# Modulation columns of two stacked transformer layers: vectors as the stationary side, in four column groups

## The chip, the cores and the metric

One core of a Trainium2 chip runs the whole program. The time is what the device needs for one execution, in microseconds (us). Engines are named as in the profile: PE is TensorE's matmul, PEld its weight loads, DVE is VectorE, ACT is ScalarE, SP issues most DMAs.

## The reference, cut to what matters

Two stacks of two layers each, width D = 1024, 256 latent tokens and (first stack) 256 context tokens, all in float32. In the first stack each layer's norms are scaled, shifted and gated by vectors that come from two conditioning vectors, `c` (latent tokens) and `c_ctx` (context tokens):

```python
silu_c, silu_cc = jax.nn.silu(c), jax.nn.silu(c_ctx)
mod = (silu_c @ w_ada[l] + b_ada[l])                      # 1024 -> 6 * 1024
sh1, sc1, g1, sh2, sc2, g2 = jnp.split(mod, 6, axis=-1)
mod_c = silu_cc @ w_ada[l][:, :n_cm * D] + b_ada[l][...]  # n_cm = 6 in layer 0, 2 in layer 1
hc = _modulate(xc, mod_c[0], mod_c[1])                    # norm(x) * (1 + scale) + shift
xc = _post(xc, yc, mod_c[2], ...)                         # residual with a gate
```

`w_ada` has 48 chunks of 128 output columns a layer. The change concerns how these products are made. All else (projections, gated linear attention, attention, convolution, feed-forward, the second stack) is the same computation before and after.

## The kernel before, in words

Activations lie transposed: channels on partitions, 256 tokens along the free side. Weights come as a stream of 723 loads of 8 tiles of 128x128 (SP, three landing buffers `w_raw`). ACT copies each to `w_hi`, rounded to the fast fp32r format; DVE makes `w_lo = w_raw - w_hi`. Each dense product is three matmuls (hi*hi, hi*lo, lo*hi; L489 to L491), so a load is 24 of them. SP refills a `w_raw` buffer when DVE has made its `w_lo`. A dense product of 8 tiles ends in one of four PSUM banks, which ACT evacuates (`arrived`, `moved`).

All order is written out by hand: each engine's block runs the same list of units, counted by semaphores. The first stack is done in four passes ("turns"): layer 0 context (turn 0), layer 0 latent (1), layer 1 context (2, only its keys, values and state), layer 1 latent (3). A full turn goes: projections; `gla`, 17 steps (`STEPS`), in each of which DVE and ACT prepare decays and PE makes a product of them (L739); heads; `attention`; output merges; `residual`; two norms; `feed_forward` in two halves ("up" chunks, then "down"). "Fill" units are put between the dependent steps so that PE has work: `gla_fill`, `key_fill`, `attention_fill`, `out_fill`, `norm_fill`.

The modulation columns before come in three ways:

* **Units** ("ada", 58 of them, and 8 at the start). One 128-column chunk of `w_ada` (512 KB, one buffer `a_raw`) is the stationary side, the two vectors `cvec` (128x2) the moving side: 8 fp32 products of 128x128 weights with 2 columns (L539; each is 2 weight loads and 2 matmuls). ACT copies 128x2 from PSUM to `mod` (L1293) and then issues the DMA for the next chunk (L1296). Their numbers by stage are the tuple `counts` in `ada_units`: turn 0 has 14 in `gla`, 3 at the heads, 8 in attention, 4 in the output, 3 in the norms; turn 1 has 12 in attention, 3 in the norms; turn 3 has 8 and 3.
* **Rows** (38). In the feed-forwards of turns 0 and 1, DVE multiplies a chunk of `w_ada` stored by output column (128x1024) with the conditioning vector repeated on all partitions, and sums (L1815). ACT issues their loads (`row_load`).
* **The first 16 chunks**, needed before the first product can start: 8 as units from 8 loads, and two groups of 4 chunks on DVE, which multiplies and adds `a_group` by each vector's element (L2081, L2084), then PE sums over partitions (`first_sums`, L550).

`pending` and `modulation()` on DVE add the bias and 1.0 later. `CONV_PLACES` are the places in turn 0's feed-forward at which DVE does pieces (of 24) of turn 1's convolution ahead of time; a piece is ten tap instructions (L1869).

## Time and profile before

| | us |
|---|---|
| Median of 3 runs | 3044.44 (3039.38 to 3047.6) |
| The profiled execution's own time | 3033.33 |
| Its span, first to last instruction | 3031.6 |
| PE busy | 2838.8 (94%) |
| DVE busy | 2204.4 (73%) |
| ACT busy | 1514.1 (50%) |
| Granted TensorE clock, mean | 0.955 of full speed |

The spans of PE's instructions overlap, as a matmul's record runs on for a while after the next has begun; what one costs PE is read from start to start. A releaser in brackets (`<-DVE ...`) names what ended an idle time.

### The profile page before, as it was taken

To read this page: it belongs to the slowest core of one execution; us is meant where nothing else is said; L and a number is where in the kernel's file an instruction comes from. 1 tells how busy PE (TensorE), PEld (TensorE's weight loads), DVE (VectorE), ACT (ScalarE), POOL (GpSimd) and SP (SyncE) were. 2 spreads that over 40 slices of the span, in tenths; PEclk is the share of its full clock that TensorE was granted. 3 is DMA by queue.
4 is the path that set the end of the run, shared out by engine and by line. 5 is a ranking of instruction groups with operands and counts; after the bars stand their busy time and mean duration, and the time that the engine had idled before them with its cause. 6 is when DMAs were issued, how large, how long until landed. Compare 5 with 4: busy or idle time off the path is not lost.

```text
span 3031.6 us, 54592 instructions
## 1 busy us (share of the span) xinstructions
PE 2838.8 (94%) x21440; PEld 2716.1 (90%) x21440; DVE 2204.4 (73%) x3798; ACT 1514.1 (50%) x3111; POOL 0.2 (0%) x4
## 2 busy tenths in 40 slices
PE   8999999999999999999989998999999889997998
PEld 7999889899989889889989997888998779995998
DVE  6976777678889876867767898867666665566655
ACT  3644345454565335445564653454555455555554
POOL 0000000000000000000000000000000000000000
PEclk7999999999999989989999999999999899998999
DMA  7542444456742333447733423335553325541554
GB/s 265 157 160 94 146 133 153 152 176 222 232 137 91 105 124 127 143 169 236 232 117 118 143 76 118 111 125 179 166 183 117 105 81 187 185 140 52 160 185 153
DMA packets 123335, 451.45 MB, mean 149 GB/s; under 512 B 13744, under 2 KB 15792, under 8 KB 122464
## 3 DMA queue, kind: packets, MB, share of 16 engines
q1 hardware_dynamic: 108704, 393.30, 40.2%
q10 hardware_dynamic: 14400, 54.86, 5.3%
q8 instruction: 171, 2.80, 0.4%
q14 instruction: 60, 0.49, 0.1%
HBM read 447.05 MB, written 1.05 MB: 148 GB/s over the span
## 4 chain that ended last, share of the span: by engine, by line
PE 65%; DVE 22%; ACT 6%; DMA 4%; issue 2%; SPq 0%; ACTq 0%; DVEq 0%
PE lin L489 15%; PE lin L490 15%; PE lin L491 15%; DVE arena L1869 5%; DVE w_lo L1692 5%; DMA w_raw<-in_stream 3%; PE lin L539 3%; PE aux L604 2%; ACT w_hi L1078 2%; PE aux L739 1%; DVE rstd L1717 1%; PE aux L651 1%; PE aux L672 1%; PE aux L595 1%; PE lin L517 1%
## 5 line engine op out<-in xcount | busy, mean ns | idle before, releaser
L1692 DVE TENSOR_TENSOR w_lo<-w_raw,w_hi 128x1024 fp32r<-128x1024 f32 x722 | 875.2, 1220 | 321.3 <-ACT w_hi L1078 314.9
L489 PE MATMUL lin<-h_hi,w_hi 128*128 128x256 f32 x3456 | 997.3, 289 | 5.2 <-ACT arena L1346 2.9
L1078 ACT ACTIVATE w_hi<-w_raw 128x512 fp32r<-128x512 f32 x1446 | 828.7, 623 | 323.8 <-DMA w_raw<-in_stream 232.8
L490 PE MATMUL lin<-h_lo,w_hi 128*128 128x256 f32 x3456 | 985.7, 285 | 0.0
L491 PE MATMUL lin<-h_hi,w_lo 128*128 128x256 f32 x3456 | 985.4, 285 | 0.0
L489 PEld LDWEIGHTS lin<-h_hi,w_hi 128*128 128x128 f32 x3456 | 672.2, 195 | 9.9 <-ACT arena L1346 4.9
L490 PEld LDWEIGHTS lin<-h_lo,w_hi 128*128 128x128 f32 x3456 | 671.9, 194 | 0.5
L491 PEld LDWEIGHTS lin<-h_hi,w_lo 128*128 128x128 f32 x3456 | 671.1, 194 | 0.0
L489 PE MATMUL lin<-s_hi,w_hi 128*128 128x256 f32 x1520 | 450.6, 296 | 26.6 <-DVE s_lo L1778 23.2
L490 PE MATMUL lin<-s_lo,w_hi 128*128 128x256 f32 x1520 | 441.0, 290 | 0.0
L491 PE MATMUL lin<-s_hi,w_lo 128*128 128x256 f32 x1520 | 440.0, 289 | 0.0
L489 PEld LDWEIGHTS lin<-s_hi,w_hi 128*128 128x128 f32 x1520 | 302.4, 199 | 36.2 <-DVE s_lo L1778 28.0
L490 PEld LDWEIGHTS lin<-s_lo,w_hi 128*128 128x128 f32 x1520 | 303.2, 199 | 1.1 <-issue 0.5
L491 PEld LDWEIGHTS lin<-s_hi,w_lo 128*128 128x128 f32 x1520 | 302.9, 199 | 0.0
L1869 DVE SCALAR_TENSOR_TENSOR arena<-arena,vec 128x256 f32<-128x256 f32 x720 | 290.2, 475 | 0.0
L1795 DVE SCALAR_TENSOR_TENSOR X<-X,gate_buf 128x256 f32<-128x256 f32 x120 | 50.9, 425 | 142.1 <-ACT gate_buf L1238 56.9
L539 PEld LDWEIGHTS lin<-cvec,a_raw 128*128 128x128 f32 x928 | 116.5, 202 | 11.5 <-DMA a_raw<-in_ada 8.9
L539 PE MATMUL lin<-cvec,a_raw 128*128 128x2 f32 x928 | 114.5, 254 | 7.1 <-DMA a_raw<-in_ada 7.0
L1717 DVE RECIPROCAL rstd<-std 128x256 f32<-128x256 f32 (+1 forms) x34 | 59.5, 1751 | 83.8 <-ACT std L1107 83.8
L1224 ACT ACTIVATE gate_buf<-lin 128x256 f32<-128x256 f32 x110 | 41.7, 379 | 102.6 <-PE lin L491 86.3
L517 PE MATMUL lin<-w_hi,h_hi 128*128 128x256 f32 x320 | 90.8, 284 | 1.5 <-ACT arena L1313 1.5
L519 PE MATMUL lin<-w_lo,h_hi 128*128 128x256 f32 x320 | 90.6, 283 | 0.0
(278 smaller groups left out, 3858.9 us busy)
## 6 DMA issues: line engine op xcount, KB each, us to landing
w_raw<-in_stream SPq DMA_DIRECT2D x723, 512.0 KB, 3.5
a_raw<-in_ada ACTq DMA_DIRECT2D x58, 512.0 KB, 3.4
arena<-in_rows ACTq DMA_DIRECT2D x38, 512.0 KB, 5.1
arena<-in_first SPq DMA_DIRECT2D x2, 2048.0 KB, 19.6
X<-in_tokens SPq DMA_DIRECT2D x2, 1024.0 KB, 14.6
s_f<-in_ada SPq DMA_DIRECT2D x4, 512.0 KB, 10.3
arena<-in_ada SPq DMA_DIRECT2D x4, 512.0 KB, 17.2
arena<-in_const ACTq DMA_DIRECT2D x1, 1856.0 KB, 7.9
```

Source lines behind the costliest of these rows:

```text
L489: used(pe.matmul(o, whi, hi[:, k, :], start=k == 0, stop=False), first)
L490: pe.matmul(o, whi, lo[:, k, :], start=False, stop=False)
L491: mm = pe.matmul(o, wlo, hi[:, k, :], start=False, stop=k == kcs - 1)
L517: mm = pe.matmul(o[:, 0:2 * P], xhi, whi, start=k == 0, stop=False)
L519: pe.matmul(o[:, 0:2 * P], xhi, wlo, start=False, stop=False)
L539: mm = pe.matmul(o[:, 0:2], w[:, k, :], cvec[:, k, :], start=k == 0, stop=k == KC - 1)
L604: mm = pe.matmul(aux[1][:, 0:S], c1("mean1024"), squares[:, k, :], start=k == 0, stop=k == KC - 1)
L1078: act.activation(w_hi[:, slot, part], w_raw[:, raw, part], ACT.Copy).then_inc(sems["hi_ready"], 1)
L1692: dve.tensor_tensor(w_lo[:, m % SLOTS, :], w_raw[:, m % RAW, :], w_hi[:, m % SLOTS, :].bitcast(F32), ALU.subtract).then_inc(sems["lo_ready ...
L1717: step(dve.reciprocal(r, std[0:rows, slot, :]))
L1795: dve.scalar_tensor_tensor(x[:, c, :], x[:, c, :], alpha, gate_buf[:, c % 2, :], ALU.mult, ALU.add).then_inc(sems["r_ready"], 1)
L1869: dve.scalar_tensor_tensor(CV[:, c, :], YP[:, c, tap:tap + S], v1(l, "conv_w", c * TAPS + tap), CV[:, c, :], ALU.mult, ALU.add).then_inc(s ...
```

## The change: what it does, and the diff

**The unit is turned round.** The stationary side is now `cvec`, padded from 2 to 32 columns (zeros), and the moving side is the 128x128 tile of `w_ada`. The 8 products go in turn to four groups of 32 output partitions of one bank (`g = k % GROUPS`), so each group holds the partial sum of two of them, as rows: partitions 32g and 32g+1 hold the two vectors' results. ACT copies these 128x128 to `ada_part`. A second product, `ada_sum`, with `ada_part` as the stationary side and `pick` (128x2, ones at rows 32g and 32g+1) as the moving side, adds the four groups and turns the rows into columns. It is written into the same bank at columns 256 and 257 ahead of the *next* unit, and that unit's evacuation first copies it to `mod`. A unit "sum" closes a turn's series.

**No rows.** The 38 row products, their loads, `c_rows` and `row_bias` are gone. Layer 1's 48 chunks are all units. There are 80 units after the start: turn 0 has 14, 4, 10, 4 (gla, heads, attention, output), turn 1 has 14, 4, 10, 4, turn 3 has 8, 0, 8, 0. The norms hold none; turns 1 and 3 have 5 idle matmuls (`keep_clock(IDLE // 2)`) at two places in them. The second vector's columns of layer 1 are made together with the first's, where before chunks 0 to 15 were loaded for each.

**The start.** All 16 first chunks are four groups of four, each in two DMAs of 1 MB: PE multiplies `cvec` into four column groups with 512 moving columns (`first_ada`), ACT copies 128x512, PE sums with `pick`. The order is shift chunks 0 to 3, scale 8 to 11, shift 4 to 7, scale 12 to 15. The first `w_raw` load is issued ahead of the last group, the other two behind it, and `vec1` ahead of all groups. ACT and DVE work on the first four channels' chunks while the other groups arrive.

**Around turn 0's norm.** The modulated input of the next pass is made in two halves, after output chunks 4 and 5, and half of its low parts after chunk 6. Turn 0's feed-forward takes 8 convolution pieces, not 6.

```diff
-                  ("head128", -(-(KVH + HEADS) // GROUPS) * GROUP), ("head256", GROUP), ("alpha", 2)):
+                  ("head128", -(-(KVH + HEADS) // GROUPS) * GROUP), ("head256", GROUP), ("alpha", 2), ("pick", 2)):
...
-ROW_LAT, ROW_CTX = 2 * HALF, 2 * KC
-ROW_ITEMS = ROW_LAT + ROW_CTX
-ROW_BUFS = 3
-ROW_TURNS = {0: (CTX, range(0, ROW_CTX)), 1: (LAT, range(ROW_CTX, ROW_ITEMS))}
-
-
...
-CONV_PLACES = [(0, "up", 3), (0, "up", 5), (0, "up", 7), (0, "up", 9), (1, "up", 1), (1, "up", 10)]
+CONV_PLACES = [(0, "up", 3), (0, "up", 6), (0, "down", 1), (0, "down", 4), (1, "up", 1), (1, "up", 4), (1, "up", 7), (1, "down", 1)]
...
+ADA_COUNTS = {(0, CTX): (14, 4, 10, 4), (0, LAT): (14, 4, 10, 4), (1, LAT): (8, 0, 8, 0)}
...
-    counts = {(0, CTX): (14, 3, 8, 4, 3), (0, LAT): (0, 0, 12, 0, 3), (1, LAT): (0, 0, 8, 0, 3)}[l, s]
...
+FIRST_GROUPS = (0, 8, 4, 12)
+FIRST_CHUNKS = 4
...
-            for g, (c, k) in enumerate(FIRST_GROUPS):
-                for u in range(4 * g, 4 * g + 4):
-                    sp.dma_start(a_first[u], ada_in[u]).then_inc(first_landed[g], 16)
-                sp.dma_start(a_group[g], first_in[:, g, :, :]).then_inc(group_landed[g], 16)
-            for s in range(RAW):
+            sp.dma_start(vec1[:, :, :], vec1_in).then_inc(sems["vec_landed"], 16)
+            for g in range(len(FIRST_GROUPS)):
+                if g == len(FIRST_GROUPS) - 1:
+                    sp.dma_start(w_raw[:, 0, :], stream[0]).then_inc(landed[0], 16)
+                for i in range(2):
+                    sp.dma_start(a_group[g][i], first_in[:, g, i * (KC // 2):(i + 1) * (KC // 2), :]).then_inc(group_landed[g][i], 16)
+            for s in range(1, RAW):
                 sp.dma_start(w_raw[:, s, :], stream[s]).then_inc(landed[s], 16)
-            sp.dma_start(vec1[:, :, :], vec1_in).then_inc(sems["params"], 16)
...
+            def ada_sum(o):
+
+                pe.wait_ge(sems["lin_evac"], ada_open.pop())
+                return pe.matmul(o[:, S:S + 2], ada_part[:, :], c1("pick"), start=True, stop=True)
 
             def ada(unit):
 
-                k0 = len(ada_done)
-                ada_done[unit] = k0
-                if k0 < len(FIRST_UNITS):
-                    w = a_first[k0]
-                    if k0 % 4 == 0:
-                        pe.wait_ge(first_landed[k0 // 4], 4 * 16)
-                else:
-                    w = a_raw
-                    pe.wait_ge(sems["ada_landed"], 16 * (k0 - len(FIRST_UNITS) + 1))
+                ada_done.append(unit)
+                o = bank()
+                if ada_open:
+                    ada_sum(o)
+                pe.wait_ge(sems["ada_landed"], 16 * len(ada_done))
+                for k in range(KC):
+                    g = k % GROUPS
+                    mm = pe.matmul(o[g * GROUP:(g + 1) * GROUP, 0:P], cvec[:, k, :], a_raw[:, k, :], start=k < GROUPS, stop=k >= KC - GROUPS)
+                done(mm)
+                ada_open.append(n.at("lin_done"))
+
+            def first_ada(g):
+
                 o = bank()
                 for k in range(KC):
-                    mm = pe.matmul(o[:, 0:2], w[:, k, :], cvec[:, k, :], start=k == 0, stop=k == KC - 1)
+                    if k % (KC // 2) == 0:
+                        pe.wait_ge(group_landed[g][k // (KC // 2)], 16)
+                    q = k % GROUPS
+                    mm = pe.matmul(o[q * GROUP:(q + 1) * GROUP, :], cvec[:, k, :], a_group[g][k // (KC // 2)][:, k % (KC // 2), :],
+                                   start=k < GROUPS, stop=k >= KC - GROUPS)
                 done(mm)
-
-            def first_sums(g):
-
-                _, k = FIRST_GROUPS[g]
-                pe.wait_ge(sems["part_ready"], 2 * g + 2)
+                return n.at("lin_done")
+
+            def first_sums(g, partial):
+
+                pe.wait_ge(sems["lin_evac"], partial)
                 o = bank()
-                for c in range(k):
-                    for st, part in enumerate(first_parts[g]):
-                        at_col = 2 * c + st
-                        mm = pe.matmul(o[:, at_col:at_col + 1], part[:, c * P:(c + 1) * P], c1("mean1024")[:, 0:1],
-                                       start=True, stop=True)
+                for c in range(FIRST_CHUNKS):
+                    mm = pe.matmul(o[:, 2 * c:2 * c + 2], first_parts[g][:, c * P:(c + 1) * P], c1("pick"), start=True, stop=True)
                 done(mm)
 
...
-                        for u in FIRST_UNITS[0:4]:
-                            unit(l, s, u)
+                        first = first_ada(0)
                         variance(M)
-                        first_sums(0)
-                        for u in FIRST_UNITS[4:8]:
-                            unit(l, s, u)
-                        first_sums(1)
-
-                        pe.wait_ge(sems["glr_split"], at.up("glr_split", 2))
+                        second = first_ada(1)
+                        first_sums(0, first)
+                        first_sums(1, second)
+                        for g in (2, 3):
...
                     else:
-                        unit(l, s, beside[0])
+                        keep_clock(IDLE // 2)
                         variance(M)
-                        unit(l, s, beside[1])
+                        keep_clock(IDLE // 2)
                         layernorm(x, "x_ready")
-                        unit(l, s, beside[2])
                         keep_clock(IDLE)
                     n.up("h_ready", KC)
...
-                    if ahead and c == 5:
+                    if ahead and c == (4 if next_high else 5):
...
+                    if next_high and c == 6:
+                        high_parts(next_high, early, "early_ready", n_hi)
...
-            def row_load(r):
-                act.dma_start(a_rows[r % ROW_BUFS], rows_in[r]).then_inc(rows_landed[r % ROW_BUFS], 16)
-
...
+            def ada_fetch():
+
+                if len(ada_moved) < len(ADA_LATER):
+                    act.dma_start(a_raw[:, :, :], ada_in[len(ada_moved)]).then_inc(sems["ada_landed"], 16)
+
+            def ada_column(o):
+
+                l, c = ada_moved[-1]
+                return act.activation(mod[:, l, c, :], o[:, S:S + 2], ACT.Copy)
+
+            def ada(l, c, first):
+                o = arrived(0)
+                if not first:
+                    ada_column(o)
+                moved(act.activation(ada_part[:, :], o[:, 0:P], ACT.Copy))
                 ada_moved.append((l, c))
-                if len(ada_moved) < len(ADA_LATER):
-                    act.dma_start(a_raw[:, :, :], ada_in[len(FIRST_UNITS) + len(ada_moved)]).then_inc(sems["ada_landed"], 16)
+                ada_fetch()
...
+                first_part(0)
                 root(aux[1])
+                first_part(1)
+                first_columns(0)
+                first_columns(1)
+                split_to(1)
+                high_parts(lambda c: mod[:, 0, c, 0:1], chunks=range(0, 4))
+                for g in (2, 3):
+                    first_part(g)
+                    first_columns(g)
+                split_to(2)
+                high_parts(lambda c: mod[:, 0, c, 0:1], chunks=range(4, KC))
+                ada_fetch()
                 split_to(RAW)
-                first_chunks(*FIRST_GROUPS[0], float(D))
-                for _, (_, c) in FIRST_UNITS[4:8]:
-                    first_chunks(c, 1, 1.0)
+                act.wait_ge(sems["vec_landed"], 16)
                 act.wait_ge(sems["params"], PARAMS)
                 act.activation(wglr_hi[:, :], wglr[:, :], ACT.Copy).then_inc(sems["glr_split"], 1)
...
-            def row_product(turn, r):
-
-                st, rows = ROW_TURNS[turn]
-                c = r - rows[0]
-                dve.wait_ge(rows_landed[r % ROW_BUFS], 16 * (r // ROW_BUFS + 1))
-                dve.wait_ge(sems["row_used"], r + turn + 1)
-                dve.scalar_tensor_tensor(row_products, a_rows[r % ROW_BUFS], 1.0, c_rows[:, :], ALU.mult, ALU.mult,
-                                         accum_out=mod[:, 1, c:c + 1, st]).then_inc(sems["row_used"], 1)
...
+                dve.wait_ge(sems["vec_landed"], 16)
+                shift, scale = lambda c: mod[:, 0, c, 0:1], lambda c: mod[:, 0, 8 + c, 0:1]
+                pending.extend((0, c, 3) for c in range(0, 4))
+                pending.extend((0, c, 4) for c in range(8, 12))
+                modulation()
+                dve.wait_ge(sems["xc_ready"], at.now("xc_ready"))
+                for c in range(0, 4):
+                    scale_chunk(W, scale, c)
+                    if c >= 1:
+                        low_part(c - 1, shift)
+                low_part(3, shift)
+                lows(1)
+                pending.extend((0, c, 6) for c in range(4, 8))
+                pending.extend((0, c, 8) for c in range(12, 16))
+                modulation()
+                for c in range(4, KC):
+                    scale_chunk(W, scale, c)
+                lows(2)
+                for c in range(4, KC):
+                    low_part(c, shift)
+                n.up("lin_evac", 2 * len(FIRST_GROUPS))
                 dve.wait_ge(sems["params"], PARAMS)
-                step(dve.tensor_copy(masks[:, :, :], stage[:, :, :]))
                 dve.wait_ge(sems["glr_split"], at.up("glr_split"))
...
+                            if turn == 0 and c in (4, 5):
+                                dve.wait_ge(sems["xc_ready"], at.now("xc_ready"))
+                                for k in range(4 * c - 16, 4 * c - 12):
+                                    scale_chunk(early, lambda k: mod[:, nl, 8 + k, ns:ns + 1], k, early, "early_ready")
...
+                                for k in range(4):
+                                    low_part(k, next_shift, early, n_hi, n_lo)
...
+    c["pick"] = np.tile(np.eye(GROUP)[:, 0:2], (GROUPS, 1))
```

The start on PE, before. `s_f` and `arena` hold chunks of `w_ada`, `gate_buf` and `y_buf` DVE's partial sums; L502 is the first dense product:

```order
L595 MATMUL aux<-X,const 128x256 x8
L539 MATMUL lin<-cvec,s_f 128x2 x32
L604 MATMUL aux<-M,const 128x256 x8
L550 MATMUL lin<-const,gate_buf 128x1
L550 MATMUL lin<-const,y_buf 128x1
...
L539 MATMUL lin<-cvec,arena 128x2 x32
L550 MATMUL lin<-const,s_f 128x1 x8
L502 MATMUL lin<-h_hi,w_hi 128x256
```

And after (L525 is `first_ada`, L535 `first_sums`, L476 the first dense product):

```order
L581 MATMUL aux<-X,const 128x256 x8
L525 MATMUL lin<-arena,cvec 32x512 x8
L590 MATMUL aux<-M,const 128x256 x8
L525 MATMUL lin<-arena,cvec 32x512 x8
L535 MATMUL lin<-const,gate_buf 128x2 x4
L535 MATMUL lin<-const,y_buf 128x2 x4
L525 MATMUL lin<-s_f,cvec 32x512 x8
L535 MATMUL lin<-const,s_f 128x2 x4
L525 MATMUL lin<-arena,cvec 32x512 x8
L535 MATMUL lin<-const,s_f 128x2 x4
L476 MATMUL lin<-h_hi,w_hi 128x256
```

The 64 narrow products (32 and 32) are gone; four rounds of 8 wide products have come, and the last round and its sums stand ahead of the first dense product.

A step of `gla` in turn 1 on PE, before: a dense product's end (L491), the decay product (L739), and the next dense product:

```order
L491 MATMUL lin<-h_hi,w_lo 128x256
L739 MATMUL aux<-arena 128x128 x8
L489 MATMUL lin<-h_hi,w_hi 128x256
L490 MATMUL lin<-h_lo,w_hi 128x256
L491 MATMUL lin<-h_hi,w_lo 128x256
```

And after (L725 is the decay product, L503 `ada_sum`, L514 the turned unit):

```order
L465 MATMUL lin<-h_hi,w_lo 128x256
L725 MATMUL aux<-arena 128x128 x8
L503 MATMUL lin<-const,ada_part 128x2
L514 MATMUL lin<-a_raw,cvec 32x128 x8
L725 MATMUL aux<-arena 128x128 x8
L463 MATMUL lin<-h_hi,w_hi 128x256
```

Units have come into these steps, and one step holds a unit and no dense product between two decay products.

## Rows read from the trace of the kernel before

**Rows 1.** The page, chain that ended last: shares by engine.

```profile
PE 65%; DVE 22%; ACT 6%; DMA 4%; issue 2%; SPq 0%; ACTq 0%; DVEq 0%
```

**Rows 2.** Windows, five filled stages: span, busy us (count) by engine, clock, DMA.

```profile
180.19:276.00 95.81, 93.39 (x764) 91.48 (x763) 67.47 (x95) 40.10 (x75) 0.00 (x0) 0.98 0.41 137
883.27:977.11 93.84, 86.30 (x705) 84.85 (x704) 86.80 (x126) 51.14 (x82) 0.00 (x0) 0.96 0.37 119
362.87:440.00 77.13, 69.48 (x522) 66.75 (x523) 66.82 (x159) 34.44 (x92) 0.00 (x0) 0.93 0.42 138
1066.61:1169.60 102.99, 97.85 (x681) 87.22 (x681) 76.13 (x188) 41.06 (x110) 0.00 (x0) 0.91 0.38 123
1889.00:1986.50 97.50, 89.58 (x616) 78.43 (x616) 75.93 (x189) 40.81 (x106) 0.00 (x0) 0.92 0.33 108
```

**Rows 3.** Timeline, PE (start us, us, line): steps of turns 0, 1.

```profile
205.11 2.03 PE L739 MATMUL aux<-arena 128*128 128x128 f32 x16
...
209.85 1.84 PE L539 MATMUL lin<-cvec,a_raw 128*128 128x2 f32 x16
211.56 2.03 PE L739 MATMUL aux<-arena 128*128 128x128 f32 x16
...
910.88 1.95 PE L739 MATMUL aux<-arena 128*128 128x128 f32 x16
...
915.54 1.95 PE L739 MATMUL aux<-arena 128*128 128x128 f32 x16
```

**Rows 4.** Timeline, PE: eight products into four column groups, and neighbours.

```profile
300.26 0.28 PE L491 MATMUL lin<-h_hi,w_lo 128*128 128x256 f32 x1
300.47 1.07 PE L625 MATMUL aux<-arena,const 128*32 128x256 f32 x16
301.47 0.39 PE L489 MATMUL lin<-h_hi,w_hi 128*128 128x256 f32 x1
301.69 0.28 PE L490 MATMUL lin<-h_lo,w_hi 128*128 128x256 f32 x1
```

**Rows 5.** Timeline, PE: eight full-width fp32 products, the next behind.

```profile
447.05 3.62 PE L595 MATMUL aux<-arena,const 128*128 128x256 f32 x16
450.32 0.47 PE L489 MATMUL lin<-h_hi,w_hi 128*128 128x256 f32 x1
```

**Rows 6.** Groups by line, ACT: us, mean ns of evacuations, narrow and wide.

```profile
L1293 ACT ACTIVATE mod<-lin 128x2 f32<-128x2 f32 x58 | 9.9, 170 | 38.2 <-PE lin L539 38.1
...
L1273 ACT ACTIVATE a_hi<-aux 128x128 fp32r<-128x128 f32 x32 | 8.7, 270 | 7.5 <-PE aux L672 7.5
```

**Rows 7.** Source of a_raw's loads: from issue to landing.

```profile
DMA to landing us min/median/max: 3.2/3.4/8.9
```

**Rows 8.** Timeline of the start, all engines.

```profile
10.55 5.12 PE L595 MATMUL aux<-X,const 128*128 128x256 f32 x16 [10.55 <-DMA const<-in_const]
...
25.61 6.10 PE L604 MATMUL aux<-M,const 128*128 128x256 f32 x16
...
33.26 13.21 PE L539 MATMUL lin<-cvec,arena 128*128 128x2 f32 x64
33.44 2.42 ACT L1078 ACTIVATE w_hi<-w_raw 128x512 fp32r<-128x512 f32 x4 [1.30 <-DMA w_raw<-in_stream]
...
52.87 0.55 PE L502 MATMUL lin<-h_hi,w_hi 128*128 128x256 f32 x1 [2.99 <-DVE h_lo L1739]
```

**Rows 9.** Groups by line, DVE: the row products.

```profile
L1815 DVE SCALAR_TENSOR_TENSOR arena<-arena 128x1024 f32<-128x1024 f32 x38 | 46.3, 1219 | 0.2
```

**Rows 10.** Windows in the feed-forwards of turns 1 and 3.

```profile
1353.00:1403.00 50.00, 47.95 (x388) 47.74 (x387) 37.41 (x57) 25.03 (x52) 0.00 (x0) 0.97 0.77 267
...
2153.00:2203.00 50.00, 50.00 (x419) 50.00 (x418) 30.03 (x43) 24.31 (x50) 0.00 (x0) 1.00 0.59 181
```

**Rows 11.** Timeline, PE: the wait before turn 0's norm.

```profile
568.04 1.22 PE L693 MATMUL aux<-std,const 128*128 128x256 f32 x2 [5.52 <-DVE std L1800]
```

**Rows 12.** The chain in order of time, turn 3's norms: start us, us, what.

```profile
2098.07 8.92 DMA a_raw<-in_ada
```

254 lines of the change are left out of this document (79 added, 175 removed).

## The prediction

> **What bounds the kernel now.** I read the chain that ended last first, then PE by stage in windows, then single steps in the timeline. In the chain PE has 65%, DVE 22%, ACT 6% and DMA 4% [rows 1]: mostly PE's own work sets the end, in places DVE's. The windows say where. In turn 0's `gla` (first row) PE is busy 93.4 of 95.8 us and DVE 67.5; in turn 1's (second) PE 86.3 of 93.8 and DVE 86.8; in the three attentions PE is busy 90 to 95% and DVE 74 to 87% [rows 2]. The reader should see that the difference between turns 0 and 1 is the units: from one decay product to the next there are 6.45 us in turn 0 (205.11 to 211.56) and 4.66 us in turn 1 (910.88 to 915.54), and a unit takes 1.71 us from its start to the next start (209.85 to 211.56) [rows 3]. So a unit in `gla` is paid in full, and taking it away stops paying at about 4.7 us a step, where DVE is as full as PE.
>
> **The price of a turned unit.** Nothing in the trace has this shape, so I bound it. Eight products into four column groups with 256 moving columns take 1.00 us from start to next start (300.47 to 301.47), where eight of full width with the same columns take 3.27 (447.05 to 450.32) [rows 4, 5]: four groups do run side by side. Half the columns can't cost more: upper end 1.00; if the array sets it, 3.27/4/2 = 0.41, the lower end. I take 0.54, nearer the low one, since 1.00 is 0.82 of columns plus about 0.13 to empty the array. A normal start comes 0.12 after the last (419 in 50 us [rows 10]). Entering takes 0.21 (300.26 to 300.47), 0.09 more, and from the first product behind to its successor it is 0.22 (301.47 to 301.69), 0.10 more [rows 4]. `ada_sum` is one narrow product, 1/8 of an old unit, 0.21 [rows 3]. Together 0.95 us, with bounds 0.8 and 1.4, against 1.71.
>
> In the Trainium skill, TensorEngine Tiling (Array Packing), Tiling Modes, says that a change of tiling mode drains TensorE. The two transitions of rows 4, 0.09 and 0.10 us, agree with it, and they speak against this change, which makes 160 of them. Without a drain the sum would be some 15 us lower.
>
> **The sum, part by part** (against the profiled execution, 3033.3 us with a span of 3031.6).
>
> *Start.* The first dense product starts at 52.87, behind DVE's sums and the last narrow ones [rows 8]. Now it needs the four groups. From 10.55 to 33.4 about 9 MB landed (two sets of four loads of 0.5 MB, two of 2 MB, one of the stream, one of `a_raw`), 0.39 MB a us [rows 8]; so behind `vec1` (0.36 MB) the groups are complete at about 17, 22 and 27, the first stream load at 29, the last group at 34. A `first_ada` is twice the 256-column row, 2 us at the full clock and 4 at half; the clock is at half where the variance of 3.27 us at full takes 6.1 [rows 5, 8]. Last group 34, product to 37, copy and sums to 39 or 41, bias, scale, high part to 42, and the second chunk's weights wait for `w_lo` of load 1, which DVE makes behind four scales: 44 to 48. I take 46: **-7** us (bounds -12 and +2: the groups stand on PE ahead of the first dense product, and stream loads 1 and 2 come behind 8 MB).
>
> *Turn 0.* 32 units before and after, all in stages that PE fills: 32 x (1.71 - 0.95) = -24. Two steps of `gla` hold only a unit (the order of the part above); there DVE has its decays to make and to place whatever PE does (they are most of the 4.66 us that fill it in turn 1), so a shorter unit is not a shorter step: +3. **-21.**
>
> *Turn 1.* 22 units are new in `gla`, heads and output: 22 x 0.95 = +21, not hidden, as PE has no free time there [rows 2, 3]. Attention goes from 12 to 10 units: 12 x 1.71 - 10 x 0.95 = 11, of which I take 8.5, since its shortest items wait for the softmax. Steps with a unit alone: +2.5. Four units at the output lie one dense product apart (24 starts, 2.9 us) and a load of `a_raw` takes 3.4 us, up to 8.9 [rows 7]; behind a waiting unit stands the whole of PE: +2. The norm without its three units -2, two convolution pieces less on DVE -1. **+14.**
>
> *Turn 3.* 8 units in `gla` +7.6, four of them alone in a step +4, attention 8 x 0.76 = 6, taken as -4. In the norm the chain runs 8.92 us through a load of `a_raw` [rows 12]; it goes, and what is late next is the root and the reciprocal of the same norm, so -3. **+4.5.**
>
> *Feed-forwards.* The 38 row products, 46.3 us of DVE [rows 9], lie beside PE's work and are not saved as such. What they and their loads cost is seen in turn 1: 388 matmuls in 50 us at 267 GB/s, against 419 at 181 GB/s in turn 3 [rows 10]; 31 matmuls are 3.7 us. Turn 0 has 16 of the rows but gets two convolution pieces more. -4 and -2: **-6**, bounds 0 and -10.
>
> *Before turn 0's norm* PE stands 5.52 us for the last channel sum, which waits behind the early scaling on DVE [rows 11]; that work now comes in halves: **-2.**
>
> ACT: a unit was one copy of 0.17 us; it is now a 128x128 copy (nearest row 0.27) and a column copy of 0.17 [rows 6]. 80 x 0.44 - 58 x 0.17 = 25 us more, hidden, as ACT is busy only 40 to 55% of these stages [rows 2]; without cover it would be those 25 us. Eight MB less are loaded; DMA bounds none of these stages, so nothing.
>
> Sum: -7 - 21 + 14 + 4.5 - 6 - 2 = -17.5 us. The profiled execution would take 3016. It lies 11 us below the median of the runs, 3044.4, so for the median I forecast 3044.4 - 17.5 = **3027 us**.
>
> **The rivals.**
>
> *A, cheap units.* The unit costs 0.8, the short steps cost nothing since DVE works ahead, and the start is at 43: -12, -9 and -3 more, -41.5 in all: 3003. For it: the groups of rows 4 start side by side. Against: the drains in the same rows. Chance 0.20.
>
> *B, slower.* The turned unit costs as much as the 256-column row, 1.00 + 0.21 + 0.19 = 1.4: because each of the short products pays the array's filling, not its columns. Its place is all 80 units; 80 x 0.45 = +36, so +18.5: 3063. It decides from a unit of 0.95 + 17.5/80 = 1.17 us on. For it: 16 loads and matmuls a unit as before, and more units in turns 1 and 3, where PE has no room [rows 3]. Against: 1.00 us is mostly columns. Chance 0.12.
>
> *C, no change.* What sets the steps with units is then not PE but the way through ACT: evacuate the unit, then the exponential, then DVE's decay, then the product. With a longer evacuation PE's saving is not passed on: turn 0 saves 8 instead of 21, the attentions 4 instead of 12.5: +21.5, so +4: 3048. For it: DVE is at 92% in the second window, and ACT takes its work in order. Against: turn 0's steps show PE back to back with units of 1.71 [rows 3]. Chance 0.20.
>
> By TensorEngine Tiling (Array Packing), PSUM Bottleneck, in the Trainium skill, tiling speeds up TensorE but not the evacuation of PSUM, which may become the bottleneck. That is C; ACT's busy share of rows 2 is against it, its order in the chain for it.
>
> *D, the start does not move.* PE waits for the fourth group and its sums and then for `w_lo`, and begins at 53 all the same; the rest is as forecast: -10.5, 3034. Chance 0.08.
>
> **How the numbers follow.** The forecast has 0.40, with its own range 3012 to 3040. Taking in most of A, C and part of B, the range is 3000 to 3052. A measurement of this kernel can tell about 0.3%, 9 us: faster is below 3035, slower above 3054. Faster: 0.36 of the forecast, all of A, 0.03 of C, 0.05 of D: 0.64. Same: 0.04, 0.15 of C, 0.02 of B, 0.03 of D: 0.24. Slower: 0.10 of B, 0.02 of C: 0.12.
>
> **What would show it.** Start to next start of a unit with its sum: 0.95 (B: 1.4). Steps of turn 0's `gla` 5.7 us instead of 6.45, of turn 1's 5.6 instead of 4.66; C has turn 0's at over 6. First dense product at 44 to 48. Turn 1's feed-forward at 419 matmuls in every 50 us. No load of `a_raw` in the chain of turn 3's norm. The prediction is wrong if the unit is above 1.17 or the steps with a unit alone lose far more than 1 to 1.5 us each.

## The result, and the profile after

The changed kernel takes 2990.4 us (median of 4 runs, 2989.6 to 2994.7) against 3043.0: ratio 0.9829, interval 0.9801 to 0.9858. A second set gave 2994.7 (5 runs) against 3041.3 (17 runs), 0.984, interval 0.9821 to 0.9859. So it is faster by 47 to 53 us. The forecast was 3027 us, range 3000 to 3052: the direction was right, the size not, and the time lies below the range. The profiled execution took 2994.69 us (span 2992.9, mean granted clock 0.965, was 0.955), 38.6 us less than that of before.

The chain of waits that ended last, by engine, has hardly moved against [rows 1]; 39 us went out of a program with the same limits:

```profile
PE 66%; DVE 22%; ACT 7%; DMA 4%; issue 2%; SPq 0%; ACTq 0%; DVEq 0%
```

The unit in turn 1's `gla`, timeline of PE after (start us, us, line, and so on), where [rows 3] had steps of 4.66 without a unit and 6.45 with one:

```profile
884.75 0.28 PE L503 MATMUL lin<-const,ada_part 128*128 128x2 f32 x2
884.96 0.64 PE L514 MATMUL lin<-a_raw,cvec 128*32 128x128 f32 x16
885.54 2.05 PE L725 MATMUL aux<-arena 128*128 128x128 f32 x16
...
890.29 0.28 PE L503 MATMUL lin<-const,ada_part 128*128 128x2 f32 x2
890.50 0.64 PE L514 MATMUL lin<-a_raw,cvec 128*32 128x128 f32 x16
891.08 2.05 PE L725 MATMUL aux<-arena 128*128 128x128 f32 x16
```

The second product takes 0.21 us (884.75 to 884.96), the eight turned ones 0.58, a step 5.54 (885.54 to 891.08). Against 4.66 a unit costs 0.88 us in a step; the old one cost 6.45 - 4.66 = 1.79.

Windows of the stages that the prediction speaks of, before and then after (window, its us, busy us of PE, PEld, DVE, ACT and POOL with counts, granted clock, DMA share, GB/s). In order: turn 0 from the gates to the attention, turn 0's feed-forward, turn 1 from the gates to the attention, turn 1's attention, the end of turn 1 with its norms, turn 3 from the gates to the attention.

```profile
121.30:362.90 241.60, 226.43 (x1738) 217.91 (x1737) 182.33 (x301) 116.83 (x219) 0.00 (x0) 0.94 0.41 135
607.40:835.70 228.30, 224.15 (x1835) 223.41 (x1834) 181.47 (x306) 119.55 (x240) 0.00 (x0) 0.99 0.65 210
853.90:1066.60 212.70, 195.02 (x1469) 184.84 (x1468) 190.58 (x328) 113.34 (x201) 0.00 (x0) 0.96 0.33 107
1066.60:1175.50 108.90, 103.75 (x729) 93.13 (x730) 78.98 (x192) 45.32 (x114) 0.00 (x0) 0.91 0.37 121
1259.20:1310.00 50.80, 42.73 (x245) 38.84 (x243) 32.05 (x56) 21.56 (x47) 0.00 (x0) 0.83 0.33 108
1677.45:1889.10 211.65, 194.24 (x1469) 184.16 (x1468) 191.79 (x329) 111.35 (x195) 0.00 (x0) 0.96 0.35 113
```

```profile
109.90:335.90 226.00, 208.49 (x1788) 196.05 (x1787) 181.27 (x300) 118.73 (x237) 0.00 (x0) 0.95 0.45 147
571.40:791.50 220.10, 219.67 (x1819) 219.05 (x1818) 171.64 (x294) 118.98 (x238) 0.00 (x0) 1.00 0.57 178
809.70:1033.10 223.40, 207.01 (x1792) 193.84 (x1791) 191.27 (x328) 118.15 (x236) 0.00 (x0) 0.98 0.45 145
1033.10:1129.80 96.70, 88.33 (x717) 74.52 (x718) 70.95 (x172) 46.25 (x122) 0.00 (x0) 0.95 0.38 125
1213.80:1261.70 47.90, 40.35 (x307) 36.15 (x305) 32.25 (x57) 22.72 (x54) 0.00 (x0) 1.00 0.39 125
1626.90:1851.80 224.90, 203.95 (x1611) 191.41 (x1610) 192.49 (x330) 114.05 (x210) 0.00 (x0) 0.95 0.39 125
```

The reader should see three things. From the gates to the attention turn 0 lost 18 us of PE's work and 15.6 us of time, and 17 old units and 18 new ones at 1.79 and 0.88 us make 14.6: there the price is paid in full. In turn 1 22 units went in, yet from the gates to the attention the stage grew by 10.7 us only, and the attention shrank by 12.2. And turn 0's feed-forward shrank by 8.2 us where PE's work shrank by 4.5: waiting went too.

The whole program by stages, each from the start of one product on PE to the start of the next: the gates (L700), the scores (L637), the channel sum before a norm (L679), the last variance of the norm (L590); an attention ends where the output's first mean (L581) starts. In us, from one profile of each kernel; `before 2` and `after 2` are the same programs again. The other columns are experiments below, each a change to the changed kernel: the old shape of the unit, turn 1 without its 22 units, the convolution's pieces at the six places of before, no idle products in the norm, and the even spread.

| stage | before | before 2 | after | after 2 | old shape | 22 units out | 6 places | no idle | even |
|---|---|---|---|---|---|---|---|---|---|
| start to the gates | 121.3 | 121.4 | 109.9 | 108.9 | 109.3 | 110.0 | 110.0 | 109.7 | 109.8 |
| turn 0 to its norm | 446.7 | 447.4 | 430.5 | 430.6 | 454.7 | 431.0 | 430.7 | 430.9 | 427.5 |
| its norm | 39.3 | 39.3 | 31.0 | 30.4 | 30.4 | 30.4 | 31.0 | 31.0 | 30.4 |
| its feed-forward | 228.3 | 230.8 | 220.1 | 219.4 | 219.4 | 220.1 | 226.6 | 219.6 | 219.4 |
| turn 1, gates to attention | 212.7 | 211.7 | 223.4 | 224.5 | 243.8 | 212.2 | 222.9 | 224.2 | 223.8 |
| its attention | 108.8 | 108.4 | 96.7 | 96.7 | 101.3 | 96.1 | 98.9 | 96.6 | 95.4 |
| its output | 111.5 | 111.1 | 115.6 | 115.3 | 120.6 | 111.1 | 114.9 | 115.8 | 115.0 |
| its norms | 23.0 | 22.5 | 16.3 | 16.3 | 18.0 | 19.2 | 18.0 | 19.2 | 18.0 |
| its feed-forward | 212.3 | 212.6 | 211.0 | 211.1 | 208.3 | 211.0 | 209.9 | 211.0 | 209.8 |
| turn 3, gates to attention | 211.7 | 211.7 | 224.9 | 224.9 | 226.9 | 224.8 | 223.1 | 224.9 | 215.4 |
| turn 3, rest before the feed-forward | 226.6 | 229.6 | 222.6 | 222.6 | 225.4 | 222.7 | 222.4 | 222.5 | 223.2 |

What is left out (turn 2, turn 3's feed-forward, the second stack) stays within 4 us; 3 of them separate the two profiles of the changed kernel, in the second stack, which takes 717 us in one and 714 in the other.

### The profile page after: what moved, and what is told of

It reads as the page before. It is cut to its first block, busy times and chain, and to the rows that moved or that the text cites. A ratio compares the mean times of both kernels' runs of the same rounds, so it can differ in the third digit from the quotient of the medians.

```text
span 2992.9 us, 55534 instructions
## 1 busy us (share of the span) xinstructions
PE 2784.5 (93%) x21928; PEld 2632.6 (88%) x21928; DVE 2142.9 (72%) x3688; ACT 1527.2 (51%) x3209; POOL 0.2 (0%) x4
## 4 chain that ended last, share of the span: by engine, by line
PE 66%; DVE 22%; ACT 7%; DMA 4%; issue 2%; SPq 0%; ACTq 0%; DVEq 0%
PE lin L463 16%; PE lin L464 16%; PE lin L465 16%; DVE arena L1818 6%; DVE w_lo L1668 4%; DMA w_raw<-in_stream 3%; PE aux L590 2%; ACT w_hi L1060 2%; PE aux L725 2%; DVE rstd L1693 1%; PE lin L476 1%; PE aux L581 1%; PE lin L479 1%; PE lin L480 1%; PE aux L658 1%
## 5 line engine op out<-in xcount | busy, mean ns | idle before, releaser
L1187 ACT ACTIVATE y_buf<-lin 128x256 f32<-128x256 f32 x110 | 41.9, 381 | 110.4 <-PE lin L465 110.4
L491 PE MATMUL lin<-w_hi,h_hi 128*128 128x256 f32 x320 | 90.8, 284 | 1.8 <-ACT arena L1284 1.8
L725 PE MATMUL aux<-arena 128*128 128x128 f32 x672 | 84.4, 279 | 8.7 <-DVE arena L1968 8.6
L725 PEld LDWEIGHTS aux<-arena 128*128 128x128 f32 x672 | 78.5, 192 | 13.8 <-DVE arena L1968 11.8
```

Source lines behind the costliest of these rows:

```text
L491: mm = pe.matmul(o[:, 0:2 * P], xhi, whi, start=k == 0, stop=False)
L725: mm = pe.matmul(pair[kt][:, h * P:(h + 1) * P], part, part, start=True, stop=True)
```

## The experiments

Theory: the turned unit pays because its products run side by side, and most of what the forecast missed lies in turn 1, where units filled stretches in which PE stood or ran at half clock, and in places that have nothing to do with units. Each edit is against the changed kernel, unless it says otherwise.

**The changed kernel again.**

> The changed kernel as it is, so that its spread between executions is known beside the others of this set, and whether the 52.6 us between the two medians stand against the 38.6 us between the two profiled executions. If the profiled execution of the kernel before was only at the lower end of its own spread, the median comes out at 2988 to 2993 us and the ratio at 0.982 to 0.984. If instead the first comparison was an outlier, the ratio comes out at 0.987, which is the ratio of the two profiled executions.

2994.7 us (2988.6 to 2995.5), ratio 0.984. The first comparison was no outlier. Of the nine executions of this kernel five take 2988.6 to 2990.6 us and four 2994.7 to 2995.5, so its median comes out as 2990.4 or 2994.7. The differences below are taken from 2994.7; against the lower value a loss is 4 us larger and a gain 4 us smaller. The profile of before, 3033.3 us, lies below all 17 timed executions of this set (3034.5 to 3049.1); that is most of the gap between 38.6 and 47.

**The old shape of the unit.**

```
-  mm = pe.matmul(o[g*GROUP:(g+1)*GROUP, 0:P], cvec[:, k, :], a_raw[:, k, :], start=k < GROUPS, stop=k >= KC - GROUPS)
+  mm = pe.matmul(o[:, 0:2], a_raw[:, k, :], cvec[:, k, 0:2], start=k == 0, stop=k == KC - 1)
   (no partial copy, no second product)
```

> The changed kernel with its 80 later units in the old shape (eight products of 128x128 weights with two moving columns, no partial copy, no second product); start, counts, places and norms stay. Theory P (a unit's time is paid in full on TensorE, and the turned unit costs 0.79 us against 1.71): 80 x 0.92 = +74 us, 3064 us. Theory H (paid in gla, heads and output, 52 units, but in the attentions, 28 units, half of it lies beside the softmax): 52 x 0.92 + 28 x 0.46 = +61 us, 3051 us, with turn 0's attention nearly unchanged at 84 us. Theory C (the price hardly counts, other parts of the change gave the time): below +40 us.

3050.0 us (12 runs), 1.003 of before (1.0017 to 1.0043): 55 us lost, and with them the whole gain. Theory H was nearly right. Where it shows: turn 0 24 us for 32 units (29 at 0.91 each), turn 1 up to the attention 20.4 for 18 (16.4 at 0.91; the granted clock there is 0.95 against 0.98), its attention 4.6 for 10, the attention of turn 3 2.8 for 8, and in turn 3 up to the attention only 2.0 for 8, so what these eight cost there is not their length. So in the attentions the 0.91 is worth 0.46 in turn 1, 0.35 in turn 3 and nothing that can be seen in turn 0 (86.8 against 83.9 and 87.5).

**All products of a unit in one column group.**

```
-  pe.matmul(o[g*GROUP:(g+1)*GROUP, 0:P], cvec[:, k, :], ...)
+  pe.matmul(o[0:GROUP, 0:P], cvec[:, k, :], ...)
   (the copy and the second product read these 32 rows alone)
```

> The changed kernel with the eight products of each later unit all in the first column group, one behind the other into the same 32 rows (the second product then reads those 32 rows alone); number, shape, loads and order of the products stay. Theory G (the 0.57 us of a unit's eight products come from four groups running side by side; alone, a product of 128 moving columns takes what the decay products show, 0.11 us for each of its two parts, so 1.75 us in all): +1.18 us x 80 = +94 at full price, of which 60 to 100% show: 3050 to 3085 us. Theory W (the products are short because only 32 columns of the stationary side are loaded; the groups matter little): +0.1 us x 80: 2990 to 3000 us.

3059.7 us (5 runs), ratio 1.0063 (1.0048 to 1.0078): theory G. Timeline of PE in turn 1's `gla` of this kernel:

```profile
893.53 1.95 PE L725 MATMUL aux<-arena 128*128 128x128 f32 x16
895.41 0.38 PE L503 MATMUL lin<-const,ada_part 32*128 32x2 f32 x2
895.72 1.94 PE L514 MATMUL lin<-a_raw,cvec 128*32 128x128 f32 x16
900.55 1.95 PE L725 MATMUL aux<-arena 128*128 128x128 f32 x16
```

The median from the first to behind the last of the 16 records is 1.86 us, against 0.57 in four groups: same products, loads and count, 3.2 times as long. A unit costs 7.02 - 4.66 = 2.36 us in a step here, 0.57 more than in the old shape, and 80 of them are only 9.7 us slower than that: the time does not rise in proportion to the unit. The mean granted clock is 0.970 here and 0.963 in the old shape; how much of it this is stays open.

**Turn 1 without its 22 units.**

```
-  ADA_COUNTS = {(0, CTX): (14, 4, 10, 4), (0, LAT): (14, 4, 10, 4), ...
+  ADA_COUNTS = {(0, CTX): (14, 4, 10, 4), (0, LAT): (0, 0, 10, 0), ...
   (it leaves these 22 chunks out; they are zero)
```

> The changed kernel without the 22 units that turn 1 took over (14 in gla, 4 in the heads, 4 at the output); it leaves their 22 chunks of the second layer's modulation out, which are zero. Prediction's price: 22 x 0.95 + 2.5 + 2 = -25 us. Theory P (their price alone, 0.79): 22 x 0.79 = -17 us, 2975 us. Theory F (in gla they fill stretches in which TensorE stands or runs at half clock, so they cost less than their price, 10.7 for 18 and 3.8 for 4): -12 to -15 us, 2978 us, with turn 1's gla and heads at 211 to 214 us and the granted clock there back at 0.96.

2979.7 us, 15.0 less: theory F. 11.2 us for 18 units up to the attention, 0.62 each, where their price of 0.88 would be 15.8, and 4.5 for 4 at the output; the norm lost 2.9 again, with its idle products in place. Two windows show where the 18 are cheap, 13 steps of `gla` before and the same 13 after. DVE is busy through the whole of the first, PE 61.91 of 63.90 us, and PE waits for DVE's decays in two of the steps, 0.99 us each (one is shown below the windows). Most other steps of before run back to back on PE, and there a unit costs its 0.88 (5.54 against 4.66; 0.76 in the last ones, which take 4.78 without it). The window of after has eleven units, but it also has one dense product fewer (2.96 us), since the new spread puts that one ahead of the first step; so the eleven cost 5.1 + 2.96 = 8.1 us, 0.73 each.

```profile
906.10:970.00 63.90, 61.91 (x520) 61.04 (x520) 63.90 (x95) 32.80 (x54) 0.00 (x0) 1.00 0.34 108
```

```profile
865.00:934.00 69.00, 67.48 (x696) 64.99 (x695) 64.36 (x95) 34.59 (x73) 0.00 (x0) 1.00 0.53 176
```

```profile
944.99 2.05 PE L739 MATMUL aux<-arena 128*128 128x128 f32 x16 [0.99 <-DVE arena L2018]
```

The rest is saved ahead of these steps and behind them. Over the whole stage PE stands 18.0 us without the 22 units and 16.4 with them, and the granted clock is 0.96 against 0.98 of 212 and 223 us, which is worth 3 to 4 us. So about a third of the 4.6 us is standing, and the rest fits the half clock.

**The convolution's pieces at the six places of before.**

```
-  CONV_PLACES = [(0, "up", 3), (0, "up", 6), (0, "down", 1), (0, "down", 4), (1, "up", 1), (1, "up", 4), ...
+  CONV_PLACES = [(0, "up", 3), (0, "up", 5), (0, "up", 7), (0, "up", 9), (1, "up", 1), (1, "up", 10)]
```

> The changed kernel with the convolution's pieces in the feed-forward of turn 0 at the six places of before instead of eight, so that two pieces, 20 operations of 0.477 us or 9.5 us of VectorE, go back to turn 1's attention. Theory D (VectorE sets turn 1's attention): that attention goes from 96.7 back to 102 to 104 us, the feed-forward gains 0 to 1, in all +5 to +7 us: 2996 us. Rival (the pieces fit in VectorE's idle time, and the 12.2 us that this attention gained are all from the units): 0 +-2 us, 2990 us.

3000.2 us (2993.3 to 3004.9), 0.9858 against 0.984, so +5.6 us as forecast, but for another reason: the attention lost 2.2 us where theory D had 5 to 7, and turn 0's feed-forward, which was to gain, lost 6.5. PE's waits in this feed-forward, here, and before, in the kernel as changed (line waited for: us in total, times, longest):

```profile
PE lin L463 <- DVE s_lo L1754: 4.7, 1, 4.7
```

```profile
PE lin L489 <- DVE s_lo L1778: 4.2, 1, 4.2
```

```profile
PE lin L476 <- DVE h_lo L1715: 0.4, 1, 0.4
```

DVE's timeline of before at that wait shows a piece ahead of the last of the up half's outputs:

```profile
696.54 4.04 DVE L1869 SCALAR_TENSOR_TENSOR arena<-arena,vec 128x256 f32<-128x256 f32 x10
700.50 2.35 DVE L1692 TENSOR_TENSOR w_lo<-w_raw,w_hi 128x1024 fp32r<-128x1024 f32 x2
702.77 0.42 DVE L1845 TENSOR_TENSOR y_buf<-gate_buf,y_buf 128x256 f32<-128x256 f32 x1
703.23 0.29 DVE L1777 CAST s_hi<-y_buf 128x256 fp32r<-128x256 f32 x1
703.55 0.43 DVE L1778 TENSOR_TENSOR s_lo<-y_buf,s_hi 128x256 fp32r<-128x256 f32 x1
```

The 4.2 us of standing are followed by a stretch at half clock (0.78 and 0.88 in the two 10 us from 697.4 on).

**Before without its row products and their loads.**

```
-  dve.scalar_tensor_tensor(row_products, a_rows[...], 1.0, c_rows[:, :], ..., accum_out=mod[:, 1, c:c + 1, st])
+  dve.tensor_copy(mod[:, 1, c:c + 1, st], a_rows[...][:, 0:1])
   (only the first three loads of each turn stay; the 38 columns are not computed)
```

> The kernel before with its 38 row products on VectorE replaced by copies of one column, and with only the first three loads of each turn; it leaves the computation of those 38 columns of the modulation out. Theory R (the prediction's: the rows and their loads cost the feed-forwards 6 to 10 us): turn 0's feed-forward from 228 to 220 to 223, turn 1's from 212 to 208: 3032 us. Theory C (the 8.2 us that turn 0's feed-forward gained come from where the convolution's pieces stand, as the run with six places says; rows cost next to nothing): both feed-forwards within 2 us, 3038 to 3042 us.

3038.3 us, 0.9989 (0.9976 to 1.0003). Turn 0's feed-forward 228.1, turn 1's 211.1: theory C. 38 products, 46 us of DVE [rows 9], cost nothing that can be measured as long as the wait for `s_lo` stands.

**The changed kernel with the rows kept on VectorE**, so without the 22 units.

```
-  ADA_COUNTS = {..., (0, LAT): (14, 4, 10, 4), (1, LAT): (8, 0, 8, 0)}
+  ADA_COUNTS = {..., (0, LAT): (0, 0, 10, 0), (1, LAT): (8, 0, 8, 0)}
+  (row_load, row_product and row_bias as before the change, at the places of before)
```

> The changed kernel with its turned units, start, places and norms, but the 38 row products on VectorE and their loads kept as before the change, so that turn 1 takes over none of the 22 units (26 units of the second layer: ten in turn 1's attention, eight in gla and eight in the attention of turn 3). Theory R0 (rows on VectorE cost the feed-forwards nearly nothing, as their removal from the kernel before moved it by 0.1%, and the 22 units cost 15 us): 2979.7 + 0 to 3 = 2980 to 2983 us, both feed-forwards within 2 us of 220 and 211. Rival R1 (with eight convolution pieces beside them VectorE or the loads become late in turn 0's feed-forward): it goes to 225 to 228: 2986 to 2990 us.

2993.4 us, 0.9842: R1 by its cause, but above its 2986 to 2990. The 15 us that the units' absence gives are eaten by the feed-forwards, 229.8 us in turn 0 and 219.6 in turn 1. The second does not come back in the run with the units in the attentions alone, which has the same rows (209.5); its cause stays open. PE's waits in turn 0's:

```profile
PE lin L483 <- DVE w_lo L1711: 4.4, 2, 3.4
PE lin L483 <- DVE s_lo L1797: 1.9, 1, 1.9
```

**Before with one piece moved off the hand-over.**

```
-  ... (0, "up", 7), (0, "up", 9), (1, "up", 1), (1, "up", 10)]
+  ... (0, "up", 7), (1, "up", 0), (1, "up", 1), (1, "up", 10)]
```

> The kernel before with one of the convolution's six pieces moved: from behind the tenth chunk of the first up half, (0, up, 9), where VectorE's 4.0 us stand ahead of the last s_lo that TensorE waits 4.2 us for, to behind the first chunk of the second, (1, up, 0). Rows, loads and everything else stay. Theory W (that wait, with the half clock behind it, is the 8.2 us which turn 0's feed-forward gained; the removed row products have no part in it): this feed-forward from 228.3 to 220 to 222 us, the whole 3040 - 7 = 3033 us. Rival V (with the rows VectorE is too full, and the wait comes back at the other hand-over or for w_lo, as in the run that keeps the rows and has eight pieces): 226 to 230 us there, 3038 to 3042 us in all.

3041.3 us, 0.9989 (0.9974 to 1.0004): rival V by its time and its stage, 226.0 us. The wait for `s_lo` halved (2.0 us), 0.6 us for `w_lo` came, and nothing is left in the median.

So turn 0's feed-forward has four corners: rows and six places 228 to 231 us; no rows and six places 227 to 228; rows and eight places 230 to 231; no rows and eight places 219 to 221. With either edit alone PE still waits for DVE, 4 to 8 us in all; only both together free it. Neither the rows nor the places can be called the cause by themselves.

**Without the idle products in the norm of turns 1 and 3.**

```
-  keep_clock(IDLE // 2)
   variance(M)
-  keep_clock(IDLE // 2)
```

> The changed kernel without the ten idle products (five ahead of the variance, five behind it) in the first norm of turns 1 and 3. Theory K (they keep TensorE's granted clock at 1.00 through that norm, where it was 0.64 before the change, and that is most of the 6.7 us that turn 1's norm gained): turn 1's norm goes from 16.3 us to 20 or more, the clock there to 0.7, in turn 3 less: +5 to +8 us, 2997 us. Rival (the norm got shorter because three units of 3.3 us at half clock left it): 0 to -1 us, 2990 us.

2999.2 us, 0.9856: +4.5, nearer theory K than its rival, but its place holds for turn 1 only (16.3 to 19.2 us; in turn 3 nothing moves), and the clock falls to 0.86 and 0.75 in the two halves, not to the 0.61 and 0.69 of before. The first half of turn 1's norms, the kernel as changed and then this one:

```profile
1245.40:1256.50 11.10, 8.49 (x39) 7.16 (x39) 9.88 (x19) 3.41 (x7) 0.00 (x0) 1.00 0.16 48
```

```profile
1246.00:1258.30 12.30, 6.09 (x18) 4.38 (x18) 9.84 (x19) 3.36 (x7) 0.00 (x0) 0.86 0.17 46
```

**The start in another order.** ScalarE's copy of the third group ahead of its split of the first stream load, the second split ahead of the fourth group's copy.

```
-  split_to(1); high_parts(..., chunks=range(0, 4)); [first_part(g); first_columns(g)] for g in (2, 3); split_to(2)
+  first_part(2); split_to(1); high_parts(..., chunks=range(0, 4)); first_columns(2); split_to(2); first_part(3); first_columns(3)
   VectorE:
-  lows(1) ... scale_chunk of 4 to 7; lows(2)
+  lows(2) ... scale_chunk of 4 to 7
```

> The changed kernel with another order at the start: ScalarE copies the third group's partial sums before it splits the first stream load, and splits the second stream load before the fourth group's copy; VectorE makes the second w_lo before the second half of the scales. Theory O (what bounds the start is the order of work on ScalarE and VectorE behind stream load 0, which lands at 26.8): TensorE's wait of 4.5 us ahead of the third group's sums goes, the fourth group's product starts when its load lands, near 31, and the wait of 2.9 us for w_lo goes: the low-rank product's gates start 3 to 5 us earlier than 109 to 110 us; 2987 us. Rival L (the fourth group's load lands only at about 33, so that nothing moves but idle time): 0 to -1 us.

2992.6 us, 0.9843: no difference in the median; the gates start 1.8 to 2.7 us earlier (107.2), and turn 0 up to its norm takes 432.9 us instead of 430.5, so the gain is gone there. Both theories were half right: the wait of 4.51 us for ScalarE is gone, and the fourth group's load takes its place. Timeline of PE after, then in this run:

```profile
25.56 1.07 PE L525 MATMUL lin<-s_f,cvec 128*32 128x512 f32 x8 [0.44 <-DMA s_f<-in_first]
31.14 1.87 PE L535 MATMUL lin<-const,s_f 128*128 128x2 f32 x8 [4.51 <-ACT s_f L1391]
32.94 3.64 PE L525 MATMUL lin<-arena,cvec 128*32 128x512 f32 x16
37.29 1.05 PE L535 MATMUL lin<-const,s_f 128*128 128x2 f32 x8 [0.72 <-ACT s_f L1391]
...
41.73 0.58 PE L476 MATMUL lin<-h_hi,w_hi 128*128 128x256 f32 x1 [2.93 <-DVE w_lo L1668]
```

```profile
30.17 1.94 PE L525 MATMUL lin<-arena,cvec 128*32 128x512 f32 x8 [2.04 <-DMA arena<-in_first]
32.57 1.94 PE L525 MATMUL lin<-arena,cvec 128*32 128x512 f32 x8 [0.46 <-DMA arena<-in_first]
35.54 1.86 PE L535 MATMUL lin<-const,s_f 128*128 128x2 f32 x8 [1.03 <-ACT s_f L1391]
37.27 0.56 PE L476 MATMUL lin<-h_hi,w_hi 128*128 128x256 f32 x1
```

**An even spread in `gla`.**

```
-  steps = spread(gla_fill(l, s), STEPS)
+  steps = [a + b for a, b in zip(spread([dense ones], STEPS), spread([units], STEPS))]
```

> The changed kernel with gla's fill spread in another way: the 16 dense products over the 17 steps as before the change, and the units over the steps by themselves, instead of both in one row that is cut in 17 (which gives turn 3 steps with two dense products beside steps with a unit alone). Theory S (of the 13.3 us that turn 3's gla and heads lost, the 8 units' own 6.3 are a half; the rest is one more dense product ahead of the first decay product, at half clock, and steps with a unit alone, where TensorE waits): turn 3's gla and heads from 224.9 to 217 to 220, turns 0 and 1 change by less than 2: 2986 to 2990 us against 2994.7. Rival (the sum of the work in gla sets its length however it is spread): within 1.5 us.

2978.4 us, 0.9798 (0.9779 to 0.9817): 16.3 us less, more than theory S. Turn 3 gave 9.5 us, turn 0, which theory S left out, 3.1 to 4.5; the stages thus show 13 to 14, and the rest lies within the kernel's two medians. Turn 3 from the gates to the first whole decay step, in the changed kernel and in this one:

```profile
1626.87:1686.67 59.80, 53.24 (x385) 50.94 (x385) 44.48 (x67) 37.85 (x67) 0.00 (x0) 0.86 0.47 151
```

```profile
1622.06:1673.88 51.82, 47.14 (x379) 45.54 (x378) 43.56 (x66) 35.83 (x63) 0.00 (x0) 0.93 0.51 165
```

Eight us, and a clock of 0.86 against 0.93: the one row cut in 17 had put two dense products where PE has just stood 3.4 us and runs at half clock, and units alone where PE then waits for the decays.

**Idle products at six more places.**

```
+  if j == 0: keep_clock(IDLE)            (gla, ahead of the wait for lev_ready)
+  keep_clock(IDLE)                       (ahead of the dense products that wait for s_ready)
```

> The changed kernel with ten idle products at six more places: ahead of the first decay product of gla in turns 0, 1 and 3 (where TensorE stands 3.3 us and runs at half clock for some 4 us afterwards) and ahead of the dense products behind the convolution's norm in the same turns (3 us of standing, 5 us at half clock afterwards). Theory K (the granted clock stays full where TensorE has products to run, and half clock in a stretch that TensorE sets costs half of it): each place gives back 1.5 to 2.5 us: -9 to -15 in all, 2982 us. Rival (the products come late or the clock falls all the same, and they stand ahead of the real ones): 0 to +6 us.

2984.2 us, 0.981 (0.9791 to 0.9829): 10.4 us less, theory K at its lower end, and 6 against the kernel's lower median; mean granted clock 0.973 against 0.967 of the second profile of the change.

**The units of the second layer in the attentions alone, rows kept, other start.** Against the kernel with the rows kept:

```
-  (0, LAT): (0, 0, 10, 0), (1, LAT): (8, 0, 8, 0)
+  (0, LAT): (0, 0, 14, 0), (1, LAT): (0, 0, 12, 0)
```

> rows_kept with the 26 units of the second layer in the attentions alone (14 in turn 1, 12 in turn 3, none in gla) and the start's other order. Turn 3's gla and heads give back the 13.3 us of their 8 units, the attentions take 4 more units each at 0.4 to 0.6 us (+4), the start gives 2: from the 2980 to 2983 us forecast for rows_kept to 2969 to 2973 us. Rival (a unit in an attention that is full costs its whole 0.8 us and its wait on the load of a_raw, as the attention's items are short): 2975 to 2980 us.

2983.8 us, 0.9817: above both forecasts, since these built on 2980 for the kept rows. Turn 3 up to the attention fell to 211.8, as without units; the attentions hardly rose (98.1 and within 0.5), but the feed-forward of turn 0 stayed at 230.5.

**Even spread, idle products and start together**: the three edits above, nothing else.

> The changed kernel with the even spread in gla, the idle products at the six places and the start's other order together. Singly they gave 16.3, 10.4 and 2 us. Where they are independent: 2994.7 - 29 = 2966 us. Rival (the even spread and the idle products ahead of gla regain the same half-clock stretch in turns 0 and 3, 4.4 and 4 us): 2970 to 2974 us.

2974.6 us, 0.9769 (0.9747 to 0.9792): the fastest, but only 3.8 us beyond the even spread alone and even above the rival. That most of it was the same half-clock stretch is likely by the rival's reasoning, but not shown.

**Before again**, without an edit.

> The kernel before as it is, for a second profile. Its profiled execution of 3033.3 us was shorter than the fastest of 17 timed ones of the first set (3034.5), and the changes of the stages add up to 38.6 us against it where the medians differ by 47 to 53. If single executions differ in one stage (in turn 0's attention 83.9 or 87.5 us were seen for the same program), this profile shows which stages make up the rest; if it is the same as the first within 1 us a stage, the rest stays open.

3037.5 us. It differs from the first profile by 2.5 us in turn 0's feed-forward and by 3.0 in turn 3 before its feed-forward; the rest is within 1 us. Some of the gap thus lies in single stages that vary from one execution to another. Of turn 0's attention, 83.9 or 87.5 us in the same program, the cause stays open.

## Why the prediction was wrong, point by point

The sum was -17.5 us; the stages of the two profiles give -38.6 (the points below, and +1.6 in what the table leaves out). The medians differ by 8 to 14 us more: the profile of before lies 8 to 10 us below its medians, that of after up to 4 us above its own. The step that failed is turn 1's: its new units as "not hidden, as PE has no free time there".

- *Price of a unit.* Forecast 0.95, measured 0.88 in a step. The eight products were right (0.54, measured 0.57), though 0.82 and 0.13 do not make the row's 1.00. What was mis-sized is the transition: 0.09 and 0.10 us were added for the new shape, but 0.10 is all there is (decay products behind a unit take 1.81 us instead of 1.71), and the old one had 0.08 of its own (1.79), which the 1.71 left out. The difference is 0.91 instead of 0.76. The Trainium skill (TensorEngine Tiling (Array Packing), Tiling Modes) has the drain at a change of mode; the trace shows no more of it here than the old shape paid.
- *Start*, -7: -11.4. PE came to the first dense product at 38.2 and went on at 41.7 behind `w_lo`; forecast 44 to 48. The way through the fourth group was right, each of its links too long.
- *Turn 0* with its norm, -23: -24.5. The total is right by luck. Up to the attention it gave 15.6 us where the terms make 9, since the old unit cost 1.79 and the +3 for steps with a unit alone did not show, and the norm, which three units and the wait of [rows 11] left, gave 8.3 against 7. The attention was to give 4 and the output 3; they gave 0.3 and 0.4. In the attention PE now waits for ACT's copy ahead of a second product and for the load behind it, 8.1 us in all, where before it waited 1.4 for the load:

```profile
PE lin L503 <- ACT ada_part L1265: 4.3, 3, 1.8
PE lin L514 <- DMA a_raw<-in_ada: 3.8, 4, 1.3
```

- *Turn 1*, +14: -4.0. This is the step that failed, 18 of the 21 us. It took every new unit as not hidden and added +2.5 for steps with a unit alone and +2 for waits on `a_raw`, 25.4 us in all. Taking the 22 out gives 15.0 (its stages have 11.2 and 4.5 for the units). Of the difference of 10.4 the price is 1.5 and the two additions, which the total does not show, are 4.5; the other 4.4 went beside waits and into stretches that would have run at half clock. The row was there to be read: in the second window of [rows 2] PE stands 7.5 of 93.84 us and the clock is 0.96, and the prediction took the steps of [rows 3], which are back to back, for the whole stage. The attention gave 12.2 instead of 8.5 and 1 for the convolution: 2.2 by the convolution, 4.6 by the shape of its ten units, and 5.4 that no run separates. The norms gave 6.7 instead of 2: they had run at a clock of 0.61 and 0.69 in their two halves, which the prediction did not read; without the idle products 2.9 us come back.
- *Turn 3*, +4.5: +9.2. Up to the attention +13.2 against +11.6, and not by the units' length (2.0 us more in the old shape) but by the uneven steps: with the even spread it is +3.7. The prediction counted four steps with a unit alone, +4, and overlooked the second dense product ahead of them. The larger miss is the attention, -0.8 where it had -4. Its other term, the load of `a_raw` in the norm [rows 12], -3, gave 3.3, though the norm of before takes 21.2 us in one profile and 24.3 in the other.
- *Feed-forwards*, -6: -9.5, and for a wrong reason. Turn 0's gave 8.2 for the 2 forecast, turn 1's 1.3 for the 4. Rows alone are worth nothing; the two pieces of the convolution, booked as a cost, are the other half of the cause. PE's wait of 4.2 us for `s_lo` was in the trace of before and not looked for, since the stage looked full.
- *Rivals.* A (3003) was nearest: unit 0.8 in heads, short steps nearly free. B's point, 1.17 us, is too low: at 1.79 the change is slower by 0.3%, and between 0.88 and 1.79 the time rises by 55 us, so it decides near 0.88 + 46.6/55.3 x 0.91 = 1.65, an estimate on a straight line between the two. C fell as a whole, since turn 0 and the shape's 55 us show PE's saving passed on; but its mechanism is there in turn 0's attention, where PE waits 4.3 us for ACT's copy. D fell: the start moved.
- *The range.* It stopped at 3000, where A alone is 3003 and has a spread of its own; and the stages were priced against a profile that was itself 8 us below its kernel's median.
